# Weight pieces of the routed experts split two at a time, with two groups of transposes moved

## The reference

```python
def hier_moe(h, ...):          # xf: 256 x 1024, 32 experts, one group of 8 and two experts of it per token
    for e in range(N_EXPERTS):
        hid = jax.nn.silu(xf @ w_gate[e]) * (xf @ w_up[e])          # 1024 -> 128
        y = y + combine[:, e:e + 1] * (hid @ w_down[e]).astype(f32)  # 128 -> 1024
```

## Time and profile before

| | us |
|---|---|
| median of three runs (lowest to highest) | 1413.89 (1412.27 to 1415.93) |
| the profiled execution's own time | 1412.22 |
| its span in the trace | 1410.4 |
| PE busy | 1391.6 (99%) |
| DVE busy | 1155.3 (82%) |
| ACT busy | 826.5 (59%) |

### The profile page before, as it was taken

One profiled execution on the slowest core, in us unless ns is written; L12 is line 12 of the kernel. 1 busy time (PEld: TensorE's weight loads), 2 busy tenths in 40 slices (PEclk: granted clock), 3 DMA queues, 4 the chain that ended last, 5 costly groups with the idle time before them and its releaser, 6 DMA issues.

```text
span 1410.4 us, 22152 instructions
## 1 busy us (share of the span) xinstructions
PE 1391.6 (99%) x7524; PEld 1177.9 (84%) x7524; DVE 1155.3 (82%) x2052; ACT 826.5 (59%) x1273; POOL 112.8 (8%) x129
## 2 busy tenths in 40 slices
PE   8999999999999999999999999999999999999998
PEld 6877788877888888887788888898888897888886
DVE  5996679999979788787889888759998878797886
ACT  6676566888875444567964444546444477754443
POOL 5100000000030000000000000003970000000000
PEclk9999999999999999999999999999999999999999
DMA  9955535999977666553357666457866642576661
GB/s 274 217 159 166 174 125 167 370 351 364 358 236 238 186 196 188 157 186 89 110 159 229 194 192 182 148 165 221 238 184 194 192 150 76 179 224 192 194 190 49
DMA packets 293815, 277.19 MB, mean 197 GB/s; under 512 B 12392, under 2 KB 253288, under 8 KB 293744
## 3 DMA queue, kind: packets, MB, share of 16 engines
q1 hardware_dynamic: 289920, 268.46, 62.6%
q0 software_dynamic: 3824, 7.83, 2.4%
HBM read 274.98 MB, written 1.26 MB: 196 GB/s over the span
## 4 chain that ended last, share of the span: by engine, by line
PE 83%; DVE 8%; DMA 4%; ACT 3%; issue 2%; SPq 0%; DVEq 0%; ACTq 0%
PE ps L890 18%; PE ps L790 14%; PE ps L792 13%; PE ps L791 13%; PE ps L896 11%; DVE w_lo L2570 3%; PE ps L897 3%; DMA raw<-in_w_down_dram 2%; PE ps L1656 1%; PE ps L908 1%; DMA raw<-in_w_up_dram 1%; ACT w_hi L1952 1%; PE ps L820 1%; PE ps L1476 1%; PE ps L1719 1%
## 5 line engine op out<-in xcount | busy, mean ns | idle before, releaser
L2570 DVE TENSOR_TENSOR w_lo<-raw,w_hi 128x1024 fp32r<-128x1024 f32 (+3 forms) x311 | 370.0, 1216 | 45.4 <-ACT w_hi L1952 43.2
L1952 ACT ACTIVATE w_hi<-raw 128x1024 fp32r<-128x1024 f32 (+4 forms) x309 | 317.2, 1053 | 52.2 <-PE ps L792 20.8
L890 PE MATMUL ps<-xT_both,w_hi 128*128 128x512 f32 x1120 | 282.0, 391 | 0.0
L2029 ACT ACTIVATE w_hi<-raw 128x1024 fp32r<-128x1024 f32 x198 | 207.9, 1058 | 115.1 <-PE ps L792 96.7
L890 PEld LDWEIGHTS ps<-xT_both,w_hi 128*128 128x128 f32 x1120 | 210.2, 188 | 42.0
L2575 DVE TENSOR_TENSOR w_lo<-raw,w_hi 128x1024 fp32r<-128x1024 f32 x198 | 238.3, 1230 | 2.8 <-ACT w_hi L2029 2.8
L2024 ACT ACTIVATE hid_sil<-hid_sil 128x256 f32<-128x256 f32 x87 | 36.3, 419 | 256.1 <-DVE hid_sil L2639 229.5
L896 PEld LDWEIGHTS ps<-xT_both,w_lo 128*128 128x128 f32 x1280 | 174.4, 190 | 12.2
L896 PE MATMUL ps<-xT_both,w_lo 128*128 128x256 f32 x1280 | 178.7, 282 | 0.0
L790 PE MATMUL ps<-w_hi,hid_hi 128*128 128x512 f32 x432 | 170.1, 394 | 0.5 <-issue 0.4
L792 PE MATMUL ps<-w_hi,hid_lo 128*128 128x512 f32 x432 | 168.9, 391 | 0.0
(11 more groups left out here) (501 smaller groups left out, 2232.4 us busy)
## 6 DMA issues: line engine op xcount, KB each, us to landing
raw<-in_ffn_w_gate_dram SPq DMA_DIRECT2D x88, 512.0 KB, 4.2
raw<-in_ffn_w_up_dram SPq DMA_DIRECT2D x88, 512.0 KB, 5.3
raw<-in_ffn_w_down_dram SPq DMA_DIRECT2D x88, 512.0 KB, 4.3
raw<-in_w_in_dram SPq DMA_DIRECT2D x40, 512.0 KB, 5.3
raw<-in_w_down_dram SPq DMA_DIRECT2D x40, 512.0 KB, 6.1
raw<-in_w_gate_dram SPq DMA_DIRECT2D x76, 256.0 KB, 4.5
raw<-in_w_up_dram SPq DMA_DIRECT2D x76, 256.0 KB, 5.6
raw<-in_rg_w_in_dram SPq DMA_DIRECT2D x16, 512.0 KB, 4.3
```

Source lines behind the costliest of these rows:

```text
L890: pe.matmul(o, hi[:, k, :], both[:, :, k, :], start=k == 0, stop=False)
L1952: act.activation(w_hi[0:parts, i % RING, 0:cols], raw[0:parts, i % RING, 0:cols], ACT.Copy)\
L2029: act.activation(w_hi[:, s, :], raw[:, s, :], ACT.Copy).then_inc(hi_done, 1)
L2570: dve.tensor_tensor(w_lo[0:parts, s, 0:cols], raw[0:parts, s, 0:cols], w_hi[0:parts, s, 0:cols].bitcast(F32), ALU.subtract).then_inc(lo_do ...
```

## The change

Three things are changed. In `token_pair` the transposes of the second 128 tokens come earlier: in ffn1 and ffn3 (`X_FIRST`) they stood behind steps 3, 5 and 7 and now stand behind steps 1, 3 and 5; in ffn0 they stood behind steps 4 and 7 and now stand behind steps 1 and 3. In `pair_products` the transposes of the previous pair stand ahead of `a == 2` in all pairs; before, they stood ahead of `a == 1` in all but pair 1. And from the fifth piece of the routed experts on, `hi_two` and `lo_two` split two neighbouring pieces (two neighbouring slots) by one operation of 2048 columns; each waits for both pieces and raises its counter by 2 at its end. `RING`, the loads and their waits are as they were.

```diff
                         columns(t, k, x_hi, w_lo)
-                        if t == 0 and n not in X_FIRST and k == 4:
-                            norm_group(n, 1, 0)
-                        elif t == 0 and n in X_FIRST and k in (3, 5):
-                            norm_two(n, k // 5)
-                    if t == 0:
-                        norm_group(n, 1, 1)
+                        if t == 0 and n not in X_FIRST and k in (1, 3):
+                            norm_group(n, 1, k // 2)
+                        elif t == 0 and n in X_FIRST and k in (1, 3):
+                            norm_two(n, k // 2)
+                        elif t == 0 and n in X_FIRST and k == 5:
+                            norm_group(n, 1, 1)
...
-                    if i and a == (2 if i == 1 else 1):
+                    if i and a == 2:
                         pair_transposes(i - 1)
...
+            def hi_two(i):
+                s = i % RING
+                for z in range(2):
+                    act.wait_ge(raw_in[s + z], 16 * PLAN.real[i + z])
+                act.wait_ge(used, i + 2 - RING)
+                act.activation(w_hi[:, s:s + 2, :], raw[:, s:s + 2, :], ACT.Copy).then_inc(hi_done, 2)
...
-                for q in (range(6, 9) if i else range(4, 9)):
-                    hi(pair_up(i) + q)
+                if i == 0:
+                    hi_two(V + 4)
+                    hi_two(V + 6)
+                else:
+                    hi_two(pair_up(i) + 6)
+                    if i == NV - 1:
+                        hi(pair_up(i) + 8)
...
                 if i < NV - 1:
-                    for q in range(9, 12 if i else 10):
-                        hi(pair_up(i) + q)
+                    hi_two(pair_up(i) + 8)
+                    if i:
+                        hi_two(pair_up(i) + 10)
...
+            def lo_two(i):
+                s = i % RING
+                dve.wait_ge(hi_done, i + 2)
+                dve.tensor_tensor(w_lo[:, s:s + 2, :], raw[:, s:s + 2, :], w_hi[:, s:s + 2, :].bitcast(F32), ALU.subtract)\
+                    .then_inc(lo_done, 2)
...
-                for q in (range(6, 9) if i else range(4, 9)):
-                    lo(pair_up(i) + q)
+                if i == 0:
+                    lo_two(V + 4)
+                    lo_two(V + 6)
+                else:
+                    lo_two(pair_up(i) + 6)
+                    if i == NV - 1:
+                        lo(pair_up(i) + 8)
...
                 if i < NV - 1:
-                    for q in range(9, 12 if i else 10):
-                        lo(pair_up(i) + q)
+                    lo_two(pair_up(i) + 8)
+                    if i:
+                        lo_two(pair_up(i) + 10)
```

## The result

The changed kernel takes 1454.56 us (median, 1453.12 to 1455.19) beside 1413.60 us for the kernel before on the same chip: 2.9% slower, ratio 1.029 with the interval 1.0277 to 1.0304. The forecast was 1430 us, with a range up to 1444: the sign was right, the loss of 41 us is two and a half times what was forecast. All results are compared with the kernel before, run on the same chip beside each.

A forecast was written before the change was run, and what follows sets the result against it. PE was taken as 99% busy, with DVE and the load queue also at their limit in the routed experts. Merged rounds +15.6, pair 16 +0.6, the rest 0: +16.2 on 1413.9 gives 1430 us, range 1414 to 1444.

The forecast's parts named there:

- L + 4.50 us: Routed experts: round of two up pieces; L is SP's first transfer start to last landing; 9.85 us forecast, ends 8.75 and 10.76.
- I take 5.35: Routed experts' loads: L taken as 5.35 us from the sample started at 208.58, giving turns of 9.85 us, +15.6 in sixteen.
- the upper bound of 6.26: Routed experts' loads: L from the slower sample, started at 190.88, giving a round of 10.76 us.
- the two samples: Two up pieces loaded, taken as with nothing in front: L 5.35 us from 208.58, 6.26 us from 190.88.
- the slower rival: Routed experts: loads take 6.26 us, turns 10.76, kernel +30, 1444 us; chance 0.20.
- entry and exit: Routed experts, pairs 0 and 1 and from pair 18 on: no change forecast, bounds -0.5 and +1.5 us.
- The PE work behind pair 18 is as it was: Exit of the routed experts: reason given for forecasting no change from pair 18 on.
- where PE waits: Routed experts: PE idle about 1.3 us per pair ahead of its first product, no longer ahead of the transposes.
- the reservation that the hidden remainder gets behind a late merged split: Expert transposes: hidden values' split may meet a late merged split on ACT or DVE, losing up to 2.3 us of a turn.
- openings and transposes at nothing: Openings counted 0, bounds -0.5 and +0.6 us; later expert transposes save at most 3 us, counted as nothing.
- The fit of the Trainium skill: Routed experts' loads: 2.0 us plus bytes at 436 GB/s, estimating L 4.4 us and a round of 8.9 us.
- the no-change case: Routed experts: at L = 4.25 the round is 8.75 us, +0.3 in all, about 1414 us; chance 0.17.

The follow-up runs named there:

- ring8_merged: Changed kernel with eight slots in place of six for the loaded pieces from pair 2 to pair 17, merged splits kept: 1421.57 us, ratio 1.0065.
- half_up: Changed kernel, but from pair 1 on up pieces are loaded for the first expert alone, 128 KB per transfer in place of 256: 1427.17 us, ratio 1.0094.
- ring8_aligned: Changed kernel with eight load slots from pair 1, 512 KB transfers for up pieces; six slots and single splits again from pair 17: 1413.85 us, ratio 1.0008.
- merge_only: Kernel before with the merged splits alone, transposes and openings in the old order: 1453.84 us, ratio 1.0274.

## Why the prediction was right in sign and short in size

**Right: the mechanism.** Two slots go round together, SP reloads both behind DVE's merged remainder, and the turn is the round, L + 4.50 us. The parts of the 4.50 were right: 1.92 + 0.10 + 2.29 + 0.17 = 4.48 measured. With the measured L of 6.67 the formula gives 11.17 us per turn, and 11.18 were measured. (A round is 11.26: the 0.17 us from the landing to ACT's start stood nowhere in the formula, and a shorter operation on ACT, 1.92 for 2.00, took half of it back.) Such a sum of measured parts comes out by itself; that the round sets the turn is shown by *ring8_merged* and *half_up*, where more slots and fewer bytes bring the turn down with every merged operation in place, and *ring8_aligned* leaves at most about 0.2% to anything else of the merge.

**Wrong: the step "I take 5.35: same shape, same queue, and not the slower of the two samples, since three rounds in turn keep the engines of the queue moving".** L is 6.67 us, not 5.35, and above the upper bound of 6.26 too. Under way a round has the bytes of another in front of it each time, and these cost time: with fewer of them down pieces of the same size land 1.7 us sooner (*half_up*). Of the two samples "with nothing in front of them" that is true of one alone. In front of the slower one SP had started a down piece 3.7 us earlier, which landed at 192.3, as the last of the four was started:

```profile
187.16 0.33 SPq L557 DMA_DIRECT2D raw<-in_w_down_dram  x1
...
raw<-in_w_down_dram SPq DMA_DIRECT2D x1, 512.0 KB, 5.2
```

So the sample that was set aside was the one with traffic, and the case to be forecast has more of it. Two rows under way were there as well. In the earlier trace rows a single piece takes 6.09 us from SP's start to ACT's split, and the view of the earlier trace rows has, for the transfers that land last,

```profile
raw<-in_w_up_dram SPq DMA_DIRECT2D x61, 256.0 KB, 5.6
```

SP starts the second piece's transfers 1.08 us behind the first's (304.74 and 305.82 above), its last transfer 1.55 us behind the first; either way that makes an estimated 7.2 us and a turn of 11.7. This one term is 16 x (11.18 - 9.85) = 21 us, most of what is missing.

**Wrong: the argument against the slower rival,** that at turns of 10.8 us the queue "would stand idle a fifth of the time". It does: 282 of 366 GB/s is 23% less. The mean says nothing about a burst. Two rounds that are given back one after the other meet in the queue and slow each other, and then it runs almost empty (78 GB/s). The rival itself was the right story, still 10 us short.

**Wrong: entry and exit, bounded at +1.5 together.** They are +1.44 and +4.6. With pair 18 counted as a turn its wait for a remainder is 1.40 us (the row of 432.97), and then

```profile
432.97 0.50 PE L790 MATMUL ps<-w_hi,xs_hi 128*128 128x512 f32 x1 [1.40 <-DVE w_lo L3243]
...
441.43 0.44 PE L1508 MATMUL ps<-con,hid_sil 128*128 128x128 f32 x2 [2.24 <-DVE hid_sil L3271]
```

PE's last transposes wait for the multiplication, which stands on DVE behind a merged remainder, itself 1.32 us late, and a single one. The two waits are 3.6 us of the 4.6. "The PE work behind pair 18 is as it was" left out the work of pair 18 itself.

**Half right: where PE waits.** Forecast was one wait of 1.3 us ahead of a pair's first product. There are two, ahead of the first and of the third piece (0.43 and 2.37 us in pair 7), as each pair has two merged up rounds. The pauses ahead of the transposes went as forecast, and the reservation that the hidden remainder gets behind a late merged split came true (8.2 us); what these waits cost of their own stays open (*merge_only*).

**Right: openings and transposes at nothing.** From ffn3's first product to L890 it is 1267.70 - 1260.89 = 6.81 us, in the earlier trace rows 6.84:

```profile
1260.89 0.36 PE L908 MATMUL ps<-w_hi,xT_both 128*128 128x256 f32 x1 [0.36 <-ACT xT_both L1966]
...
1267.70 1.78 PE L890 MATMUL ps<-xT_both,w_hi 128*128 128x512 f32 x7
```

**The fit of the Trainium skill** (DMA: Bandwidth & Descriptors, "Anatomy of one DMA"), from which an estimated L of 4.4 us came, is 2.3 us under this trace. It has a term for a transfer's own bytes and none for bytes of others in the queue, so it speaks for the no-change case, which did not come.

## What to carry to other kernels

In a ring whose round is as long as the consumer's turn, slots that go round together pay twice: each waits for the other's landing, and their loads start in a burst. A sample of a load is worth only as much as the traffic in front of it resembles the traffic to come. Before merging, take the time that a load needs under way from the row of one that was waited for, and add the start of the second piece's load and the longer splits; if that sum is longer than the turn times slots over pieces per turn, add slots or don't merge. The work saved is no measure of the gain: here 10.5 us less of ACT bought none of the 41 back.

## What the runs showed of the hardware that was not expected

A queue that was a quarter empty in the mean (282 GB/s) did not land its loads as if it were empty: the up transfers took 4.8 us (median), like the sample with a load in front of it, and the other sample's last one 3.8. And behind one pause the clock fell: PE stood 2.37 us ahead of the product at 310.35, and the granted clock was 0.64 from 310 to 312 us and 0.50, which is 1.2 GHz, from 312 to 314. The next products start 0.42 us apart, until 313.75, then 0.23 again:

```profile
310.35 0.62 PE L790 MATMUL ps<-w_hi,xv_hi 128*128 128x512 f32 x1 [2.37 <-DVE w_lo L3243]
310.77 0.63 PE L791 MATMUL ps<-w_lo,xv_hi 128*128 128x512 f32 x1
...
314.10 0.39 PE L790 MATMUL ps<-w_hi,xv_hi 128*128 128x512 f32 x1
314.33 0.39 PE L791 MATMUL ps<-w_lo,xv_hi 128*128 128x512 f32 x1
```

From 310.35 to 314.10 nine products take 3.75 us in place of some 2.1: 1.6 us, once in the stage. Behind a pause of 2.14 us (370.37) the clock stayed at 1.00. The length of the pause alone doesn't decide: in *merge_only* the granted clock was 0.52 from 266 to 268 us, behind a pause of 1.86 us, and stayed at 1.00 behind one of 2.25 us.
